# A decoder layer with 32 experts on one core: expert products, routing and end rearranged by pairs

## What is computed

```
h = rmsnorm(x, norm2) * (1 + sc2) + sh2
group = argmax of 4 group logits; two best of the 8 experts of that group
out[token] = sum over its two experts: weight * ((silu(h @ w1[e]) * (h @ w3[e])) @ w2[e])
x = x + g2 * out
```

## Time and profile before

| what | us |
|---|---|
| median of 3 runs | 660.89 (656.96, 660.89, 661.02) |
| the profiled execution, its own time | 655.55 |
| its span, first to last instruction | 653.8 |

### The profile page before, as it was taken

One profiled execution on the slowest core, in us unless ns is written; L12 is line 12 of the kernel. 1 busy time (PEld: TensorE's weight loads), 2 busy tenths in 40 slices (PEclk: granted clock), 3 DMA queues, 4 the chain that ended last, 5 costly groups with the idle time before them and its releaser, 6 DMA issues.

```text
span 653.8 us, 7874 instructions
## 1 busy us (share of the span) xinstructions
PE 599.4 (92%) x3008; PEld 358.0 (55%) x3008; DVE 303.9 (46%) x607; ACT 168.6 (26%) x368; POOL 97.0 (15%) x136
## 2 busy tenths in 40 slices
PE   2699799999999999999999989999999988899785
PEld 0444486877676667754788745444445433344333
DVE  0228986446666564238424474322323222236167
ACT  3025022244334434242103202222223121112010
POOL 2022241079200000000001021211111111100000
PEclk9799899999999999999999999999999999899899
DMA  8994844321763306060755754899999999999963
GB/s 313 398 355 185 336 163 161 129 69 60 266 249 127 132 18 240 15 243 2 309 219 212 292 228 186 341 418 420 419 421 420 418 421 418 420 420 422 385 259 129
DMA packets 41498, 173.85 MB, mean 266 GB/s; under 512 B 6268, under 2 KB 6332, under 8 KB 28660
## 3 DMA queue, kind: packets, MB, share of 16 engines
q1 hardware_dynamic: 34128, 159.40, 61.5%
q0 software_dynamic: 5744, 12.84, 5.4%
q10 hardware_dynamic: 1588, 1.10, 0.5%
HBM read 165.36 MB, written 15.74 MB: 277 GB/s over the span
## 4 chain that ended last, share of the span: by engine, by line
PE 65%; DMA 17%; issue 6%; DVE 6%; POOL 3%; SPq 2%; ACTq 1%; ACT 1%; DVEq 0%; POOLq 0%
DMA arena<-in_w_dram 13%; PE bank L922 11%; PE bank L645 6%; PE bank L647 6%; PE bank L646 6%; PE bank L954 5%; PE bank L735 4%; POOL ss L1887 3%; DMA qkg<-in_k_norm_dram 2%; PE bank L827 2%; PE bank L937 2%; PE bank L829 2%; PE bank L828 2%; PE bank L767 2%; PE bank L669 2%
## 5 line engine op out<-in xcount | busy, mean ns | idle before, releaser
L922 PE MATMUL bank<-arena,hT 128*64 128x512 f32 x352 | 86.9, 635 | 9.2 <-DMA arena<-in_w_dram 7.9
L645 PE MATMUL bank<-hT_high,w_in_parts 128*128 128x512 f32 x160 | 66.3, 414 | 0.0
L647 PE MATMUL bank<-hT_high,w_in_parts 128*128 128x512 f32 x160 | 62.7, 392 | 0.0
L646 PE MATMUL bank<-hT_low,w_in_parts 128*128 128x512 f32 x160 | 62.4, 390 | 0.0
L922 PEld LDWEIGHTS bank<-arena,hT 128*64 128x64 f32 x352 | 24.7, 144 | 51.3 <-issue 41.8
L1206 ACT COPY probs<-bank 128x512 f32<-128x512 f32 x32 | 18.8, 587 | 120.3 <-PE bank L922 120.3
L1616 DVE TENSOR_SCALAR hT<-bank,ab 128x128 f32<-128x128 f32 x64 | 21.9, 405 | 45.4 <-PE bank L907 45.4
L954 PE MATMUL bank<-arena,g1b 128*64 128x512 f32 x176 | 39.7, 593 | 2.6 <-DVE g1b L1631 2.6
L937 PEld LDWEIGHTS bank<-fold,probs 128*128 128x128 f32 x256 | 32.6, 196 | 16.0 <-issue 11.4
L922 PE MATMUL bank<-late,hT 128*64 128x512 f32 x160 | 36.5, 598 | 3.9 <-DMA late<-in_w_dram 3.9
L1643 DVE TENSOR_TENSOR acc<-bank,g2b 128x512 f32<-128x512 f32 x18 | 11.6, 686 | 60.2 <-PE bank L954 60.2
(11 more groups left out here) (286 smaller groups left out, 999.5 us busy)
## 6 DMA issues: line engine op xcount, KB each, us to landing
arena<-in_w_dram SPq DMA_DIRECT2D x66, 1024.0 KB, 22.9
late<-in_w_dram SPq DMA_DIRECT2D x30, 1024.0 KB, 24.2
late<-in_w_ada_dram SPq DMA_DIRECT2D x6, 2048.0 KB, 12.8
arena<-in_w_ada_dram SPq DMA_DIRECT2D x5, 2048.0 KB, 8.9
arena<-in_w_in_dram SPq DMA_DIRECT2D x4, 2048.0 KB, 11.0
late<-in_w_in_dram SPq DMA_DIRECT2D x4, 2048.0 KB, 16.7
y_scratch<-arena POOLq DMA_DIRECT2D x1, 4096.0 KB, 17.7
late<-in_w_out_dram SPq DMA_DIRECT2D x2, 2048.0 KB, 7.9
```

Of the source, the lines that this page charges most:

```text
L645: mm(bank[:, b, :], wH[:, b, k, :], hH[:, k, :], start=k == 0, stop=False)
L646: mm(bank[:, b, :], wH[:, b, k, :], hL[:, k, :], start=False, stop=False)
L647: last = mm(bank[:, b, :], wL[:, b, k, :], hH[:, k, :], start=False, stop=k == 7)
L922: last = mm(bank[r, 2 + n % 2, :].rearrange("p (w f) -> p w f", w=2), xgT[n // 2 % 2][:, k, SLOTS * (n % 2):SLOTS * (n % 2 + 1)], w13[s][: ...
```

## The change

In words, part by part:

1. Pairs. `gate_up(q)` does both experts of a pair: 16 products, expert 2q into partitions 0 to 63 and 2q+1 into 64 to 127 of one bank, each summed over all 8 steps k. The ACT copy and the fold products are gone; ACT takes tanh of the gate half of the bank (128 x 256), DVE makes the hidden tile by two 128 x 256 operations, PE transposes it (`hidden_transposes`, 2 transposes, inside the next pair's `gate_up`), ACT copies it to SBUF, and `down` reads that. `ab_done` now counts pairs, so SP releases two experts at once.
2. Routing. The logits of tile 2 come ahead of the last h2 transposes, with one constant product in place of three. Ranks are read from the bank directly; their copies come after the first one-hot tables. `gidx` comes from one operation on the copied sums, since the second column of the new constants `tokb` holds the tile's first token minus 4096. The index groups are three (pairs 0 and 1; 2 and 3; 4 to 15) in place of two. Other buffers take the tables, so that `load2(5)` follows `load13(5)` at once.
3. Ranks of odd experts run downwards: slot 64 minus rank in place of 1 plus rank.
4. End by halves. The last `down` does the columns' first half first and signals it; DVE drains each half as it comes; `add_stored` of tiles 1 to 3 moves between the adds of the spread banks. In the last pair, `down` of the pair before comes ahead of `gate_up`.
5. Three products of constants (128 x 512 each) behind each pair from q = 6 on, except the last.

The diff, cut:

```diff
-        IDX_GROUPS = [range(0, 2), range(2, PAIRS)]
+        IDX_GROUPS = [range(0, 2), range(2, 4), range(4, PAIRS)]
...
             def load_pair(e):
+                sp.wait_ge(ab_done, e // 2 + 1 - RING // 2)
                 for j in range(2):
-                    sp.wait_ge(ab_done, e + j + 1 - RING)
                     load13(e + j, (e + j) % RING)
                 sp.wait_ge(y_done, e // 2 + 1 - RING // 2)
...
             load13(5, 5)
-            sp.wait_ge(ab_done, 1)
-            load13(RING, 0)
-            sp.wait_ge(idx_psum, 2)
             load2(5, 5)
-            sp.wait_ge(ab_done, 2)
-            load13(RING + 1, 1)
-            sp.wait_ge(y_done, 1)
-            load2(RING, 0)
-            load2(RING + 1, 1)
-            for e in range(RING + 2, E, 2):
+            for e in range(RING, E, 2):
                 load_pair(e)
...
-            keep_warm(3, 7)
+            router(TT - 2)
             h2_transposes(TT - 1)
-            router(TT - 2)
+            keep_warm(1, 7)
             router(TT - 1)
...
             slot_sums(0)
-            keep_warm(7, 5)
+            keep_warm(3, 5)
+            slot_sums(1)
+            keep_warm(4, 5)
...
                 for k in range(KT):
+                    for x, s in enumerate(slots):
+                        last = mm(bank[SLOTS * x:SLOTS * (x + 1), 2 + q % 2, :].rearrange("p (w f) -> p w f", w=2),
+                                  xgT[q % 2][:, k, SLOTS * x:SLOTS * (x + 1)], w13[s][:, :, k, :],
+                                  start=k == 0, stop=k == KT - 1)
+                    if q == 0 and k == 2:
+                        gather_transposes(1)
+                    if q == 1 and k < 3:
+
+                        slot_sums(2, IDX_GROUPS[2][4 * k:4 * k + 4])
+                    if 1 <= q < PAIRS - 1 and k == 3:
+                        hidden_transposes(q - 1)
                 last.then_inc(ab_done, 1)
...
+            def step(q):
+                if q == PAIRS - 1:
+
+                    hidden_transposes(q - 1)
+                    down(q - 1)
+                    gate_up(q)
+                    return
+                gate_up(q)
+                if q >= 1:
+                    gather_transposes(q + 1)
+                    down(q - 1)
+                if q >= PAIRS // 2 - 2:
+
+                    keep_warm(3, 4 + (q - 1) % 2)
...
+            ev, od = slice(0, E, 2), slice(1, E, 2)
+            v.tensor_tensor(maskf[:, :, ev], oh1[:, :, ev], oh2[:, :, ev], ALU.add)
+            link(v.scalar_tensor_tensor(out=maskf[:, :, od], in0=oh1[:, :, od], scalar=-1.0, in1=oh2[:, :, od],
+                                        op0=ALU.mult, op1=ALU.subtract))
...
+            v.scalar_tensor_tensor(out=rm[:, :, ev], in0=ranks[:, :, ev], scalar=1.0, in1=maskf[:, :, ev],
+                                   op0=ALU.add, op1=ALU.mult)
+            link(v.scalar_tensor_tensor(out=rm[:, :, od], in0=ranks[:, :, od], scalar=-float(SLOTS), in1=maskf[:, :, od],
                                         op0=ALU.add, op1=ALU.mult))
...
+                v.scalar_tensor_tensor(out=gidx[:, a:b], in0=slotv[:, a:b, 0], scalar=float(OUT_OF_BOUNDS),
+                                       in1=slotv[:, a:b, 1], op0=ALU.add, op1=ALU.add).then_inc(idx_ready, 1)
...
             one_hot(0, range(TT))
+            link(v.tensor_copy(cnt, bank[:, 7, 128:160]))
+            link(v.tensor_copy(rk, ranks))
             indices(0)
-            one_hot(1, range(0, 2))
+            one_hot(1, range(TT))
+            indices(1)
+            one_hot(2, range(0, 2))
...
             modulate_gathered(0)
-            one_hot(1, range(2, TT))
-            indices(1)
-            weights_by_slot()
+            one_hot(2, range(2, TT))
+            modulate_gathered(1)
...
+            all_pairs(step, overflow_counts, near_end)
+            dve.wait_ge(yg_loaded[0], 16)
+            add_stored(0)
+            for h in range(2):
+                drain_last(1, range(h, h + 1))
             for h in range(2):
                 y_low(1, h)
             for n in range(2 * TT):
                 t, w = n % TT, slice(CH * (n // TT), CH * (n // TT + 1))
+                if 1 <= n < TT:
+                    dve.wait_ge(yg_loaded[t], 16)
+                    add_stored(t)
                 dve.wait_ge(spread_done, n + 1)
```

More of the change, by code:

```diff
@@ L245, in hybrid_trunk @@
         maskm, oh2b = (work(TT * E // 2).bitcast(BF16).rearrange("p (t e) -> p t e", t=TT) for _ in range(2))
-        tok1, tokg = (work(PAIRS) for _ in range(2))
+        tokg = work(PAIRS)
         work = worker(route[:, :], ROUTE)
@@ L930, in fold_halves, with gate_up @@
[L930 to L935, removed]
-                    for ft in range(FT):
[L937 to L952, removed]
+            def gate_up(q):
+                slots = [(2 * q + x) % RING for x in range(2)]
+                for s in slots:
+                    pe.wait_ge(w13_loaded[s], 32 * (2 * q // RING + 1))
+                pe.wait_ge(xgT_ready, q + 1)
+                pe.wait_ge(xgT_act, q + 1)
+                if q >= 2:
+                    pe.wait_ge(hs_ready, q - 1)
+                for k in range(KT):
+                    for x, s in enumerate(slots):
[8 more added lines that the diff above has]
+                        hidden_transposes(q - 1)
+                last.then_inc(ab_done, 1)
@@ new lines, in hidden_transposes, with down @@
+            def hidden_transposes(q):
+                pe.wait_ge(hs_ready, q + 1)
+                if q >= 2:
+                    pe.wait_ge(hid_ready, q - 1)
+                for ft in range(FT):
+                    last = nc.tensor.transpose(bank[:, 4 + q % 2, P * ft:P * (ft + 1)], hs[q % 2][:, ft:F:FT],
+                                               ident[:, :])
+                last.then_inc(hT_done, 1)
+            def down(q):
+                slots = [(2 * q + x) % RING for x in range(2)]
+                pe.wait_ge(hid_ready, q + 1)
+                if q == 0:
+                    pe.wait_ge(cws_ready, 1)
+                for s in slots:
+                    pe.wait_ge(w2_loaded[s], 16 * (2 * q // RING + 1))
+                if q >= 1:
+                    pe.wait_ge(y_drained, q)
+                for h in range(2):
+                    for ft in range(FT):
@@ L979, in _ @@
             keep_warm(2, 5)
[L980 to L981 removed]
+            all_pairs(step, near_end=lambda: counts.append(overflow_count(pe)))
             pe.wait_ge(spreadT_ready, 1)
             pe.wait_ge(yL_ready, 1)
[L984 removed]
+            for n in range(2):
                 spread(STORED, n)
[L986 to L987 removed]
+            hidden_transposes(PAIRS - 1)
+            spread(STORED, 2)
+            down(PAIRS - 1)
+            for n in range(3, 6):
                 spread(STORED, n)
[L989 to L995, removed]
+            for h in range(2):
+                pe.wait_ge(y_last, h + 1)
+                spread(STORED, 6 + h)
+                pe.wait_ge(yL_ready, 2 + h)
+                for n in range(TT * h, TT * (h + 1)):
+                    spread(PAIRS - 1, n)
             def overflow(b):
@@ L1199, in modulate_gathered, with hidden_tanh, hidden_copy, step @@
                 last.then_inc(xgT_act, 1)
[L1201 to L1213, removed]
+            def hidden_tanh(q):
+                act.wait_ge(ab_done, q + 1)
+                if q >= 2:
+                    act.wait_ge(hT_done, q - 1)
+                sc.activation(hs[q % 2], bank[:, 2 + q % 2, 0:F], ACT.Tanh, scale=0.5).then_inc(th_ready, 1)
+            def hidden_copy(q):
+                act.wait_ge(hT_done, q + 1)
+                if q >= 2:
+                    act.wait_ge(y_done, q - 1)
+                sc.copy(hidT[:, q % 2].rearrange("p f s -> p (f s)"),
+                        bank[:, 4 + q % 2, 0:FT * P]).then_inc(hid_ready, 1)
+            def step(q):
+                if q == 0:
+                    modulate_gathered(1)
+                else:
+                    hidden_copy(q - 1)
+                if q == PAIRS - 1:
+                    near_end()
+                hidden_tanh(q)
+                if 1 <= q < PAIRS - 1:
+                    modulate_gathered(q + 1)
             def y_high(i, h):
@@ L1677, in near_end @@
                 counts.append(overflow_count(dve))
-                for h in range(2):
-                    y_low(0, h)
                 dve.wait_ge(tok_iota, 1)
```

135 lines of the change are left out of this document (61 added, 74 removed).

## The result

| | before | changed |
|---|---|---|
| median of 11 runs each, us | 658.9 (655.52 to 661.72) | 664.08 (662.63 to 668.45) |
| profiled execution, own time | 655.55 | 668.45 |
| its span | 653.8 | 666.7 |

The ratio is 1.010, interval 1.0074 to 1.0126: the changed kernel is 5.2 us slower in the median. (One of the nine executions of run 9 further down took 3360.61 us, for no cause that a trace shows, and is left out of its ratio.) The two profiled executions lie at the opposite ends of their kernels' runs, 12.9 us apart, so the stretches have to be compared one by one. I use six marks: the last residual add of the projection, the copy of the logits (logits), the first product of an expert (first gate_up), the first release of w2 to the ring (the unbroken stream), the end of the last gate_up, the end of the span.

A forecast was written before the change was run, and what follows sets the result against it. DMA was taken to bound the pair loop. Stream +0.5, late start +2.7 and tail about -0.8 made +2.4 on 653.8: span 656.2, plus 1.75 gives 658.0 us, range 650 to 665.

The forecast's parts named there:

- The bound and the stream: Pair loop: bound by weight DMA at 418 to 422 GB/s, 16.35 us a pair; stream end taken +0.5 us later.
- the step that failed: Router ahead of routing: reordering gives nothing, since the removed constants (2.77 us for three) were filling a wait.
- the tables: From gidx to first modulation: work put on DVE eats up the shorter routing; first product at 393.9, cost +0.9 us.
- Part 1: Pair loop: PE takes 11.95 us a pair, 1.5 less, worth nothing behind a stream of 16.35.
- Part 3: End of stream: odd ranks downwards gain 0 of 6 to 7 us engine lateness; rival, they even it out, chance 0.25.
- Part 4: Tail behind the last weights: about -0.8 us, most of the gain lost to additions in line on DVE.
- Part 5: Pair loop: constants make PE 14.72 of 16.35 us, free in the stream; rival, PE becomes the bound, 670, chance 0.12.
- that 3 us goes: Last pairs: constants keep PE's idle short, removing the half-clock gate_up of 6.54 in place of 3.58 us.
- The lateness behind pair 14's constants: Last pair: its gate_up stands behind pair 14's whole step, 18.9 us against 16.2, so PE starts 2.7 late.
- The comparison with the median: Whole kernel: 658 is 0.4% under the median 660.89, 0.4% over the profiled 655.55, both no change; within 1%, chance 0.62.
- the hope that the products remove slow stretches: Tail: further half-clock stretches might explain runs near 661, and the products remove those; no separate size given.

The follow-up runs named there:

- run 9: Changed kernel with router's old order, tables behind first modulation, down(13) ahead of gate_up(14), constants behind pairs 6 to 12 and 14: 656.2 us, ratio 0.9947; again 654.26, 0.9954.
- run 8: Changed kernel, its router order kept, with three more products of constants ahead of router(2): 662.7 us, ratio 1.0083 to the kernel before.
- run 1: Changed kernel with the router's old order and its three products of constants: 661.56 us, ratio 1.0051 to the kernel before.
- run 2: Kernel before with only the router's new order: 660.52 us, ratio 1.0063 to the kernel before.
- run 5: Changed kernel with the router's old order and the two large one-hot tables behind the first modulation: 657.78 us, ratio 1.0003 to the kernel before.
- run 7: Kernel before with only the odd experts' ranks turned downwards: 658.88 us, ratio 1.0024 to the kernel before.
- run 4: Changed kernel with the odd experts' ranks upwards as before: 667.59 us, ratio 1.0143 to the kernel before.
- run 3: Changed kernel without the three products of constants behind the pairs: 663.96 us, ratio 1.0111 to the kernel before.
- run 6: Changed kernel with router's old order, tables behind the first modulation, and no constants behind pair 14: 656.32 us, ratio 0.9981 to the kernel before.

## Why the prediction was wrong, step by step

- **The bound and the stream: right.** The stream is 417 to 423 GB/s in every slice from 450 to 617 us, and from the first w2 release to the end of the last gate_up it was 215.4, forecast 214.5.
- **Part 2, the step that failed:** "The reordered router gives nothing, by my reading: `router(2)` waits for ACT's modulation, so the products of constants that go were filling a wait." The wait is there (the products even outlast it, by 1.4 us in run 8), but emptying it and turning the order were priced at 0. The two cost 5.2 us between the two profiles, and 0.5 to 0.6% (3 to 4 us) alone in either kernel (runs 1, 2). Two terms were left out: after the wait TensorE works at half clock through the router and on for some 17 us, and the last transposes' modulation loses its cover by router(2). Run 8 puts the second at 1.9 us with the three constants in place; without them it is some 0.6 by the estimate there, and the clock the rest. The prediction priced the clock at the end of the kernel and not here.
- **Part 2, the tables: right in place, sign and size.** +1.6 against +0.9 forecast, and the 0.8 above it are the constants at half clock. The price was known and accepted: moving the tables behind the modulation won 2.3 us between `gidx` and the modulation (runs 1 and 5). That and the router are the whole loss: with both mended the ratio is 1.0003.
- **Part 1:** hidden by the stream, as said.
- **Part 3: nothing, as forecast** (run 7). The swizzle rule of the Trainium skill (DMA: Bandwidth & Descriptors, The descriptor swizzle) pointed the same way; runs 4 and 7 agree with it without naming an engine.
- **Part 4: right.** Start of last gate_up to end is 31.4 against 32.0 forecast.
- **Part 5: the numbers right, the reason wrong.** The last gate_up took 7.04 at full clock, as forecast, but "that 3 us goes" was put down to the constants, and without them it takes 7.07, at full clock too (runs 3 and 6). That part of the forecast was luck: something else in the new order of the last pairs removes the stretch, and no run says what. The lateness behind pair 14's constants, forecast 2.7, was worth 1.65 when undone (run 6). Run 3 shows that the constants in the stream bring nothing measurable.
- **The comparison with the median** went the wrong way: 658 was set beside 660.89, but more runs put the kernel before at 658.9, and the hope that the products remove slow stretches had no run behind it.

## What to carry to other kernels

Products of constants in a wait are not free to remove: look at what the granted clock does in the small work that follows, and price it at half speed. Ask also what stands on the path at that moment: the same half clock costs little where it falls on constants while another engine works. When work is put ahead of a step that waits for a DMA, add up everything on that engine between the two, and move what is needed later behind it; here that was 2.3 us in the traces and about 0.5% in the ratio. In a part bound by transfers, shortening TensorE's work won nothing that could be measured.

## What the runs showed of the hardware that was not expected

- A wait of 1.25 us on TensorE behind 36-column products and ahead of more of them was followed by half clock for some 17 us, into the constants behind the logits; with three 512-column constant products in the wait the same router products ran at full clock (run 8). In the kernel before the clock fell there without any wait, behind 5.3 us of transposes and router products (366.88 to 372.14). Whether the wait or the small products bring the fall, no run separates.
- Waits in the stream, between 512-column products, did not tell by their length alone what followed. Waits of 1.86 and 2.17 us left the clock at 1.00 in the changed kernel (580 to 620 us). But one of 2.34 there (ahead of 500.71) and one of 2.17 in run 9 (ahead of 591.57) were followed by 5.35 in place of 3.65 us for 16 products, and one of 2.88 in the kernel before (ahead of 551.68) by 3.65.
- The 16 DMA engines finished the same queue of weights some 14 us apart (622 to 636 us in the changed kernel). In the run of the kernel before, the stored rows, asked for at 617.33, cover most of that fall.
